# Gate logits of the second layer computed ahead, weights stored by blocks, every sixth down row of that stretch added on DVE

## What is computed

```python
h = _rmsnorm(x, norm_mix[l])
qkv_a, z_a, a_a, b_a, qkv_b, u_c, gate_logits = _split_cols(h @ w_in[l])
o_a = deltanet(qkv_a, z_a, a_a, b_a, ...)        # branch A
o_b = dilated_window_attention(qkv_b, ...)       # branch B
o_c = pooling(u_c, ...)                          # branch C
gates = sigmoid(gate_logits)                     # 3 x 1024 columns of w_in
x = x + (sum_b gates[b] * (o_b @ w_branch[b])) @ w_out[l]
xt = _rmsnorm(x, norm_ffn[l])
# 8 heads, top 16 of 16384 experts each: expert ids and gates of a token
act = gelu(einsum('nd,nhkd->nhk', xt, w_up[expert])) * gate
x = x + einsum('nhk,nhkd->nd', act, w_down[expert])
```

## Time and profile before

| | |
|---|---|
| runs, us | 5200.92, 5194.58, 5197.1; median 5197.1 |
| profiled execution | 5199.42 us, its span 5197.6 us |
| busy | PE 87%, PEld 50%, DVE 58%, POOL 30%, ACT 24% of the span |
| DMA | 1432.07 MB in all, 276 GB/s over the span |
| mixing of layer 0, of layer 1 | about 0 to 1110 us, 2600 to 3700 us |
| expert stage of layer 0, of layer 1 | about 1110 to 2600 us, 3700 to 5197 us |

### The profile page before, as it was taken

One profiled execution on the slowest core, in us unless ns is written; L12 is line 12 of the kernel. 1 busy time (PEld: TensorE's weight loads), 2 busy tenths in 40 slices (PEclk: granted clock), 3 DMA queues, 4 the chain that ended last, 5 costly groups with the idle time before them and its releaser, 6 DMA issues. The chain is left out here.

```text
span 5197.6 us, 49535 instructions
## 1 busy us (share of the span) xinstructions
PE 4531.0 (87%) x17008; PEld 2622.0 (50%) x17008; DVE 3014.1 (58%) x7295; ACT 1221.7 (24%) x3107; POOL 1584.1 (30%) x1420
## 2 busy tenths in 40 slices
PE   8899999999889777777799999999998897777777
PEld 6866677754444322222278667777544443223221
DVE  6523323247776799965565233322576777999655
ACT  2211211022222233321222112110232222333221
POOL 0412110024444444444304121000244444444442
PEclk9999999999999999999999999999999999999999
DMA  3223243259999999999912232432699999999998
GB/s 106 82 84 117 70 139 112 89 219 412 409 412 402 420 420 419 418 415 420 378 46 81 84 124 70 145 115 82 245 414 410 408 398 420 420 419 420 418 420 339
DMA packets 331291, 1432.07 MB, mean 276 GB/s; under 512 B 27168, under 2 KB 147104, under 8 KB 183136
## 3 DMA queue, kind: packets, MB, share of 16 engines
q0 software_dynamic: 177376, 1268.07, 60.1%
q1 hardware_dynamic: 150144, 159.82, 9.5%
q10 hardware_dynamic: 3520, 1.02, 0.1%
HBM read 1399.49 MB, written 49.44 MB: 279 GB/s over the span
## 5 line engine op out<-in xcount | busy, mean ns | idle before, releaser
L2850 PE MATMUL ps<-early,diag 128*128 128x512 f32 (+1 forms) x3536 | 1661.5, 617 | 386.0 <-ACT diag L2765 385.5
L2667 POOL DMA_INDIRECT early<-in_peer,ids x884 | 995.1, 1126 | 1288.5 <-PE ps L2850 1203.4
L2694 DVE SCALAR_TENSOR_TENSOR early<-early,rows 128x1024 f32<-128x1024 f32 x884 | 1070.1, 1223 | 461.5 <-DMA early<-in_peer,ids 459.3
L2850 PEld LDWEIGHTS ps<-early,diag 128*128 128x128 f32 (+1 forms) x3536 | 644.9, 190 | 1337.3 <-issue 698.7
L2850 PE MATMUL ps<-late,diag 128*128 128x512 f32 (+1 forms) x928 | 437.3, 616 | 135.6 <-ACT diag L2765 135.5
L2765 ACT ACTIVATE diag<-consts_sb,weight 128x128 f32<-128x128 f32 (+1 forms) x1152 | 392.9, 388 | 688.5 <-DVE weight L2704 670.4
L2757 ACT ACTIVATE gel<-dot 128x2 f32<-128x2 f32 x576 | 117.4, 204 | 1285.5 <-DVE early L2694 972.9
L1295 PE MATMUL ps<-hT,gate_ring 128*128 128x288 f32 x1536 | 397.2, 414 | 11.3 <-ACT gate_out L1306 6.8
L2850 PEld LDWEIGHTS ps<-late,diag 128*128 128x128 f32 (+1 forms) x928 | 161.6, 183 | 409.6 <-ACT diag L2765 224.6
L2667 POOL DMA_INDIRECT late<-in_peer,ids x232 | 259.9, 1120 | 307.7 <-PE ps L2850 289.6
L2694 DVE SCALAR_TENSOR_TENSOR late<-late,rows 128x1024 f32<-128x1024 f32 x232 | 280.4, 1223 | 110.4 <-DMA late<-in_peer,ids 108.4
(11 more groups left out here) (386 smaller groups left out, 5570.7 us busy)
## 6 DMA issues: line engine op xcount, KB each, us to landing
gate_ring<-in_w_in POOLq DMA_DIRECT2D x48, 512.0 KB, 4.7
slot<-in_w_branch SPq DMA_DIRECT2D x16, 1152.0 KB, 6.3
ring<-in_w_in SPq DMA_DIRECT2D x8, 2048.0 KB, 9.4
late<-in_peer_query SPq DMA_DIRECT2D x32, 512.0 KB
early<-in_peer,ids POOLq DMA_INDIRECT x884
gate_rows<-gate_out POOLq DMA_DIRECT2D x48, 288.0 KB, 2.4
slot<-gate_rows SPq DMA_DIRECT2D x16, 864.0 KB, 8.2
slot<-in_w_in SPq DMA_DIRECT2D x6, 2048.0 KB, 11.2
```

The lines of the kernel that those rows point to most:

```text
L2667: pool.indirect_dma_start(place(q), None, table_rows, bass.IndirectOffsetOnAxis(ap=ids[:, n, c:c + 1], axis=0)).then_inc(s.pair[PLACE[q]], 16)
L2694: nc.vector.scalar_tensor_tensor(out=up, in0=up, scalar=1.0, in1=rows[:, n, :], op0=ALU.mult, op1=ALU.mult, accum_out=dot[:, i % 2, k:k + ...
L2850: ins = nc.tensor.matmul(g.ps[0:r, 2 * (n % 2) + m, :], diag[:, q % DIAGS, 0:r], place(q)[:, D + m * 512:D + (m + 1) * 512], start=False, ...
```

## The change

Three edits. **Blocks:** `w_in`, `w_pool`, `w_branch` and `peer_query` are handed over in blocks, so that what one load brings to a partition lies in one piece in HBM (4 KB for a gate unit or a query unit, 16 KB for a slab of 512 columns, 9 KB for a merge slot); the transposing is done before the launch. **Ahead:** the layer 1 gate logits of tokens 0 to 383 are computed in layer 0's expert stage, one unit (8 products of 384 columns) in every second group from 238 to 284, copied by ACT, loaded and stored by SP; for that `NextNorm` makes tiles 0 to 2 ready in groups 223 to 236 (tile 3 stays near 260 to 267), the places from row 244 on are ten instead of twelve, and layer 1's window stage computes only the 192 remaining columns of each unit, once per unit. **DVE adds:** of rows 479, 485, ... 569, 16 in each layer, DVE adds weight times down half to `x` (for the last tile to `own`), so ACT makes no diagonal and PE no product for them. `x` of tile 3 is added to its sum at the tile's end, `own` behind the last row.

```diff
+class GateRun:
+
+
+    def __init__(self, layer_of, halves, before):
+        self.layer, self.halves, self.before = layer_of, halves, before
+        self.per = len(halves)
+        self.total = self.per * GATE_UNITS
+
+
+AHEAD = 3 * P
+GATE_RUNS = (GateRun(0, (slice(0, HALF), slice(HALF, TOK)), 0), GateRun(1, (slice(0, AHEAD),), 2 * GATE_UNITS),
+             GateRun(1, (slice(AHEAD, TOK),), 3 * GATE_UNITS))
+RUN_AHEAD = 1
+RUN_OF = (0, 2)
+
+
 class Gates:
 
...
-        self.w = rows_of(layer(t["w_in"], l))
+        self.nc, self.g, self.number, self.run = nc, g, l, GATE_RUNS[run]
+        self.w, self.rows = layer(t["in_gate"], self.run.layer), layer(t["gate_rows"], self.run.layer)
+        self.ring, self.out, self.weights_in, self.stored = ring, out, weights_in, stored
+        self.columns = slice(self.run.halves[0].start, self.run.halves[-1].stop)
...
-        j, b = divmod(i, 3)
-        c = C_G + b * D + j * P
-        eng.dma_start(self.ring[:, i % GATE_RING], self.w[:, :, c:c + P]).then_inc(self.g.s.gate_weights[i % GATE_RING], 16)
+        eng.dma_start(self.ring[:, i % GATE_RING], self.w[i]).then_inc(self.weights_in[i % GATE_RING], 16)
...
-        eng.wait_ge(self.g.s.gate_copied, 2 * (self.l * GATE_UNITS + i + 1))
-        eng.dma_start(self.rows[i], self.out[:, i % GATE_OUT]).then_inc(self.g.s.gate_stored[i % GATE_OUT], 16)
+        eng.wait_ge(self.g.s.gate_copied, self.run.before + self.run.per * (i + 1))
+        width = self.columns.stop - self.columns.start
+        eng.dma_start(self.rows[i][:, self.columns], self.out[:, i % GATE_OUT, 0:width]).then_inc(self.stored[i % GATE_OUT], 16)
...
-                gates.project(pe, 2 * u + 1)
+                if gates.run.per == 2:
+                    gates.project(pe, 2 * u + 1)
...
-        sp.dma_start(self.weights(j), self.w_b[:, :, j * P:(j + 1) * P]).then_inc(sem, 16)
+        sp.dma_start(self.weights(j), self.w_b[j]).then_inc(sem, 16)
...
-EARLY, MIXED, LATE = 8, 2, 4
+EARLY, MIXED, LATE = 8, 2, 2
+LATE_WORDS = 4 * 2 * D
...
-EXTENDED = 236
+EXTENDED = 244
...
-GO_ON = (10, 11, 12, 13, 1, 2, 3, 4, 5, 6, 7, 0)
+GO_ON = (10, 11, 1, 2, 3, 4, 0, 5, 6, 7)
...
+ROUTES_DONE = TILE_END[TOGETHER - 1] + (len(HEADS) - 1) * 4 - TILE_END[TOGETHER - 1] // 2
+BATCHES = ((0, 1, 2), ROUTES_DONE + 3), ((3,), TILE_END[TILES - 2] + 5)
+GATES_AT = BATCHES[0][1] + 15
...
+def gates_at(i):
+
+
+    v, late = divmod(i - GATES_AT, 2)
+    return [v] if 0 <= v < GATE_RUNS[RUN_AHEAD].total and not late else []
+
+
+BY_VECTOR = [q for q in range(2 * GATES_AT, PAIRS - 6) if q % 6 == 5]
+BY_TENSOR = [q for q in range(PAIRS) if q not in BY_VECTOR]
+SUMMED = list(itertools.accumulate(0 if q in BY_VECTOR else 1 for q in range(PAIRS)))
+TILE_OF = [n for n, c0 in BY_GROUP for k in range(GROUP)]
+FIRST_SUM = min(q for q in BY_TENSOR if TILE_OF[q] == LAST_TILE - 1)
...
+            sp.wait_ge(s.pe_b, NQ)
+            sp.wait_ge(s.far_sums, NQ)
+            for i in range(GATE_RING):
+                self.ahead.load(sp, i)
...
+            for i in range(GATE_UNITS):
+                self.ahead.store(sp, i)
+            self.ahead.stored_all(sp)
             for i in range(2):
-                sp.wait_ge(s.downs_done, PAIRS - 4 + 2 * i)
+                sp.wait_ge(s.added, len(BY_VECTOR))
+                sp.wait_ge(s.downs_done, SUMMED[PAIRS - 5 + 2 * i])
...
+        for v in gates_at(i):
+            if v == 0:
+                pe.wait_ge(s.scored0, NQ)
+                pe.wait_ge(s.scored, NQ)
+                pe.wait_ge(s.far_scored, 2 * NQ)
+                pe.wait_ge(s.next_hT_a, len(BATCHES[0][0]))
+                pe.wait_ge(s.next_hT_b, len(BATCHES[0][0]))
+            self.ahead.project(pe, v, 6 + v % 2, 1 if v else 0, self.hT)
...
+            def add_own(i):
+                for q in range(i * GROUP, (i + 1) * GROUP):
+                    if q in BY_VECTOR:
+                        n, k, row = TILE_OF[q], q % GROUP, place(q)[:, D:2 * D]
+                        w = weight[:, i % 2, k:k + 1]
+                        dve.wait_ge(s.weighted, i + 1)
+                        if added_by(q) > 1:
+                            dve.wait_ge(s.added, added_by(q) - 1)
+                        if q == FIRST_OWN:
+                            last = nc.vector.tensor_scalar(own[:], row, w, None, ALU.mult)
+                        else:
+                            to = own[:] if n == LAST_TILE else g.x[:, n, :]
+                            last = nc.vector.scalar_tensor_tensor(out=to, in0=row, scalar=w, in1=to, op0=ALU.mult, op1=ALU.add)
+                        last.then_inc(s.added, 1)
...
+                if i:
+                    add_own(i - 1)
...
-                    if LAST[q] >= 0:
-                        pool.wait_ge(s.downs_done, LAST[q] + 1)
+                    if LAST[q] in BY_VECTOR:
+                        pool.wait_ge(s.added, added_by(LAST[q]))
+                    elif LAST[q] >= 0:
+                        pool.wait_ge(s.downs_done, SUMMED[LAST[q]])
...
+                    if q in BY_VECTOR:
+                        continue
...
+                if i == TILE_END[LAST_TILE - 1] + 1:
+                    pe.wait_ge(s.added, added_by(TILE_END[LAST_TILE - 1] * GROUP + 1))
+                    add_x(LAST_TILE - 1, False).then_inc(s.summed, 1)
+                if i == TILE_END[LAST_TILE]:
+                    pe.wait_ge(s.added, len(BY_VECTOR))
+                    for m in range(2):
+                        last = nc.tensor.matmul(g.ps[0:r, 2 * (n % 2) + m, :], table(g, "ident2"), own[:, m * 512:(m + 1) * 512],
+                                                start=False, stop=True)
+                    last.then_inc(s.summed, 1)
...
-            w_q = lambda u: rows_of(layer(t["peer_query"], l))[:, :, u * P:(u + 1) * P]
+            w_q = lambda u: layer(t["peer_query"], l)[u]
...
+def blocks_first(w, width):
+
+
+    shape = w.shape[:-2] + (w.shape[-2] // P, P, w.shape[-1] // width, width)
+    lead = tuple(range(len(shape) - 4))
+    n = len(lead)
+    return w.reshape(shape).transpose(lead + (n + 2, n + 1, n, n + 3))
+
```

More of the change, by code:

```diff
@@ L480, in __init__ @@
         self.ring = self.inner("ring", [P, 2, 4096])
-        w_in = layer(t["w_in"], l)
-        self.slabs = [rows_of(w_in)[:, :, i * 512:(i + 1) * 512] for i in range(4)]
+        self.slabs = [layer(t["in_delta"], l)[i] for i in range(4)]
     def first_slab(self, i):
@@ L1294, in project @@
         for k in range(KT):
-            last = nc.tensor.matmul(g.ps[:, bank, 0:HALF], self.ring[:, i % GATE_RING, k, :], g.hT[:, k, at:at + HALF],
+            last = nc.tensor.matmul(g.ps[:, bank, 0:c.stop - c.start], self.ring[:, i % GATE_RING, k, :], hT[:, k, c],
                                     start=k == 0, stop=k == KT - 1)
@@ L1301, in copy @@
         g, s = self.g, self.g.s
[L1302 to L1306, removed]
+        i, c = v // self.run.per, self.run.halves[v % self.run.per]
+        if v % self.run.per == 0 and (self.number or i >= GATE_OUT):
+            act.wait_ge(self.stored[i % GATE_OUT], 16 * (self.number * (GATE_UNITS // GATE_OUT) + i // GATE_OUT))
+        act.wait_ge(s.gate_sum, self.run.before + v + 1)
+        at = c.start - self.columns.start
+        self.nc.scalar.copy(self.out[:, i % GATE_OUT, at:at + c.stop - c.start], g.ps[:, bank, 0:c.stop - c.start]).then_inc(s.gate_copied, 1)
 AT_VALUES, AT_SLAB = AT_LATE + 1536, AT_LATE + 4608
@@ L1554, in weigh @@
                 if u:
-                    gates.project(pe, 2 * u)
+                    gates.project(pe, gates.run.per * u)
                 turn(u, 1)
-                gates.project(pe, 2 * u + 1)
+                if gates.run.per == 2:
+                    gates.project(pe, 2 * u + 1)
                 turn(u, 2)
@@ L1605, in _ @@
                         if u:
-                            gates.copy(act, 2 * u)
+                            gates.copy(act, gates.run.per * u)
                         if u + 1 < len(units):
                             exps(u + 1)
-                    elif q == 1:
+                    elif q == 1 and gates.run.per == 2:
                         gates.copy(act, 2 * u + 1)
@@ L1692, in window_samples @@
     mask = table(g, "smask")
-    first_gate = 2 * 4 * SLOTS
+    first_gate = gates.run.per * 4 * SLOTS
+    gates_left = gates.run.total - first_gate
     gate_bank = lambda i: 0 if i % 2 else 7
@@ L1700, in _ @@
             clear_other_set(pool, g)
-            for i in range(first_gate // 2 - 1, GATE_UNITS - 1):
+            for i in range(4 * SLOTS - 1, GATE_UNITS - 1):
                 gates.store(pool, i)
@@ L1797, in _ @@
             turn_sums(3)
-            for i in range(9, 2 * GATE_UNITS - first_gate):
+            for i in range(9, gates_left):
                 gate(i)
@@ L1803, in gate @@
             def gate(i):
-                gates.copy(act, first_gate + i, gate_bank(i))
+                if i < gates_left:
+                    gates.copy(act, first_gate + i, gate_bank(i))
             def exps(u):
```

(28 more changed lines are left out.)

176 lines of the change are left out of this document (107 added, 69 removed).

## The result

The changed kernel takes 5136.1 us, the median of four runs (5131.9 to 5144.1), against 5197.6 before (5194.6 to 5200.9, four runs): ratio 0.988, 95% interval 0.987 to 0.990, 61 us less. The forecast was 5129. Beside the later experiments it was timed once more: 5137.7 us, ratio 0.988 (0.987 to 0.990). Traces of kernels that share the code of layer 0's mixing show that part up to 10 us apart (1087.5 to 1097.7 us up to the first gather), so a difference of a few microseconds in a single trace is not read; it is read where the traces of several kernels agree on it.

What follows compares the result with a forecast made beforehand. Transfers were taken to bound the expert rows, PE the mixing. Terms: +41 gate transfers, +4 `own`, -56 `window_prompt`, -39 `window_samples`, -18 blocks, together -68 us, giving 5129 us; bounds 5105 to 5163 (68%), 80% range 5100 to 5178.

Runs made afterwards that it cites:

- no_loads: Changed kernel, but only the first three of the 24 weight loads of the gates ahead are made: 5120.8 us, ratio 0.986.
- one_slice_window: Changed kernel, but each of the 24 gate units in layer 1's window stage makes one of its 8 products: 5125.6 us, ratio 0.986.
- turns_first: Changed kernel, but in layer 1's prompt part PE turns all a unit's scores before its gate; ACT makes their copies, exponentials, then the gate's copy: 5106.2 us, ratio 0.982.
- no_adds: Changed kernel, but DVE adds no row, all 576 rows are PE's, and `own` and its product are gone: 5146.8 us, ratio 0.990.

## What to carry to other kernels

Moving work under a stage that another resource bounds is paid in that resource, by its bytes, and can be priced from the saturated row before it is built: 17.3 MB at 0.42 MB/us were 41 us against 93 us saved. When two resources come within a few per cent, a small relief (here every sixth row on DVE) is worth no more than the excess of the one over the other, about 15 us here, and nothing in a stage where the other binds anyway; in layer 1 it cost about 2 us. And when filler (work placed to cover another engine's time) leaves a chain, the order around the filler has to be looked at again: it was laid out to cover what now is bare, and a few moved lines gave 30 us.

## What the runs showed of the hardware

TensorE's granted clock differed between the kernels in one and the same part, and a lower clock costs time where PE is in the chain: the same code of the prompt part took 121.9 us at 0.99 (no_loads) and 129.9 at 0.92 (after). In the prompt part the mean granted clock was 1.00 with PE busy 166 of 180 us (before), 0.92 with 95 of 131 (after), 0.73 with 69 of 113 (one_slice_window), and again 1.00 with 86 of 100 (turns_first). The busy share does not settle it: no_loads, with the same code in this part, was at 0.99 with 86 of 122. The 40 products of the values took 2.40 us with the clock at 1.00 (the 2.4 GHz level), and 3.98 with a mean of 0.58 (one_slice_window), near the 1.2 GHz level. In the gate stretch, where PE waits for transfers, 0.86 instead of 0.99 cost nothing.

The busy share of the DMA engines stayed at 0.99 while their rate fell from 416 to 398 and 389 GB/s and PE was the limit (no_adds, no_loads). In a stretch like this one the rate tells more than the share.
